# A modulation front in three groups of rows on TensorE, with an extra product per unit and a reordered start

## What is computed

```python
c_act = jax.nn.silu(c)
cc_act = jax.nn.silu(c_ctx)
mod = (c_act @ ada_w[l] + ada_b[l])[:, None, :]
sh1, sc1, g1, sh2, sc2, g2 = jnp.split(mod, N_MOD, axis=-1)
h = modulate(x, sh1, sc1)            # x * (1 + sc1) + sh1
mod_c = cc_act @ ada_w[l] + ada_b[l]
hc = modulate(x_ctx, csh1, csc1)     # the context tokens, layer 0 only
y, yc = even_mixer(h, hc, ...)       # h @ w_in, hc @ w_in, then attention
```

## Time and profile before

| what | value |
|---|---|
| time, median of 3 runs | 1842.48 us (1840.47 to 1844.92) |
| the profiled execution, its time | 1838.9 us |
| its span | 1837.0 us |
| TensorE busy | 1780.8 us, 97% of the span |
| VectorE / ScalarE / GpSimd busy | 1257.7 / 896.2 / 1003.9 us |
| mean granted TensorE clock | 0.992 of full |
| moved by DMA | 346.01 MB |

### The profile page before, as it was taken

One profiled execution on the slowest core, in us unless ns is written; L12 is line 12 of the kernel. 1 busy time (PEld: TensorE's weight loads), 2 busy tenths in 40 slices (PEclk: granted clock), 3 DMA queues, 4 the chain that ended last, 5 costly groups with the idle time before them and its releaser, 6 DMA issues.

```text
span 1837.0 us, 30955 instructions
## 1 busy us (share of the span) xinstructions
PE 1780.8 (97%) x10814; PEld 1532.3 (83%) x10814; DVE 1257.7 (68%) x2222; ACT 896.2 (49%) x1507; POOL 1003.9 (55%) x431
## 2 busy tenths in 40 slices
PE   5999899998999999999999999999999999999998
PEld 2847579987988887788879799999999988888887
DVE  6587657878548877515433369978889957777776
ACT  3034744455436554443354546665555555455553
POOL 4033146444666543585438768877777744444443
PEclk8999999999999999999999999999999999999999
DMA  8787247876565555553325455544444455555554
GB/s 328 252 306 252 93 138 231 278 267 217 198 230 174 188 186 169 172 172 119 111 92 175 160 179 181 182 162 166 162 161 161 161 188 191 193 194 194 194 194 161
DMA packets 95323, 346.01 MB, mean 188 GB/s; under 512 B 10544, under 2 KB 12032, under 8 KB 94592
## 3 DMA queue, kind: packets, MB, share of 16 engines
q1 hardware_dynamic: 78048, 283.67, 45.9%
q10 hardware_dynamic: 17184, 61.11, 9.5%
HBM read 343.66 MB, written 1.08 MB: 188 GB/s over the span
## 4 chain that ended last, share of the span: by engine, by line
PE 81%; DVE 8%; DMA 4%; issue 3%; ACT 2%; POOL 2%; ACTq 0%; DVEq 0%; SPq 0%; POOLq 0%
PE ps L635 27%; PE ps L570 24%; PE ps L582 6%; PE ps L588 3%; DMA ring<-stream 2%; PE ps L705 2%; PE ps L554 2%; PE ps L791 2%; POOL ring_lo L515 2%; PE ps L1023 2%; PE ps L858 2%; PE ps L805 2%; PE ps L1290 1%; PE ps L615 1%; DVE hot_parts_b L2813 1%
## 5 line engine op out<-in xcount | busy, mean ns | idle before, releaser
L515 POOL TENSOR_TENSOR ring_lo<-ring,ring_hi 128x1024 fp32r<-128x1024 f32 x371 | 901.0, 2432 | 645.8 <-ACT ring_hi L509 644.6
L509 ACT ACTIVATE ring_hi<-ring 128x1024 fp32r<-128x1024 f32 x502 | 531.6, 1060 | 547.2 <-DMA ring<-stream 545.1
L570 PE MATMUL ps<-h_span,ring_hi 128*128 128x256 f32 x3168 | 415.9, 284 | 0.6 <-ACT ring_hi L509 0.6
L570 PEld LDWEIGHTS ps<-h_span,ring_hi 128*128 128x128 f32 x3168 | 396.4, 192 | 6.4 <-issue 4.2
L635 PE MATMUL ps<-ring_hi,e_pair 128*128 128x512 f32 x1024 | 253.6, 389 | 1.9 <-DVE e_pair L2854 1.9
L2854 DVE TENSOR_TENSOR e_pair<-arena,e_pair 128x256 fp32r<-128x256 f32 x128 | 174.6, 1364 | 100.2 <-ACT e_pair L1857 99.9
L635 PEld LDWEIGHTS ps<-ring_hi,e_pair 128*128 128x128 f32 x1024 | 192.1, 188 | 41.9 <-issue 2.3
L570 PE MATMUL ps<-h_span,ring_lo 128*128 128x256 f32 x1584 | 222.3, 283 | 0.4 <-POOL ring_lo L515 0.4
L570 PEld LDWEIGHTS ps<-h_span,ring_lo 128*128 128x128 f32 x1584 | 204.3, 192 | 0.8 <-POOL ring_lo L515 0.8
L515 DVE TENSOR_TENSOR ring_lo<-ring,ring_hi 128x1024 fp32r<-128x1024 f32 x141 | 179.2, 1272 | 37.6 <-ACT ring_hi L509 37.3
L635 PE MATMUL ps<-ring_hi,arena_r 128*128 128x512 f32 x672 | 175.8, 394 | 2.4 <-ACT ring_hi L509 2.4
(11 more groups left out here) (297 smaller groups left out, 2195.5 us busy)
## 6 DMA issues: line engine op xcount, KB each, us to landing
ring<-stream SPq DMA_DIRECT2D x540, 512.0 KB, 3.3
arena<-aside_w ACTq DMA_DIRECT2D x49, 512.0 KB, 4.6
late<-aside_w ACTq DMA_DIRECT2D x21, 512.0 KB, 4.7
resid<-aside_w ACTq DMA_DIRECT2D x10, 512.0 KB, 6.3
arena<-scale_w ACTq DMA_DIRECT2D x8, 512.0 KB, 14.7
arena<-ln_rows ACTq DMA_DIRECT2D x8, 512.0 KB, 5.3
arena<-gate_cols ACTq DMA_DIRECT2D x2, 1024.0 KB, 4.6
arena<-decay ACTq DMA_DIRECT2D x1, 1536.0 KB, 6.8
```

What stands on the lines that cost most here:

```text
L509: act.activation(ring_hi[:, s, :], ring[:, s, :], ACT.Copy).then_inc(hi_ready, 1)
L515: eng.tensor_tensor(ring_lo[:, s, :], ring[:, s, :], ring_hi[:, s, :], ALU.subtract).then_inc(lo_ready[s], 1)
L570: m = pe.matmul(ps[:, bank, 0:T], w[:, kc * P:(kc + 1) * P], x[:, kc, :], start=begin, stop=w is w_lo and kc == KC - 1)
```

## The change

It does the following, all of it in the first 60 us of the program.

- The stream has four more units of `ada_w` at its start (`EARLY_ADA` 8 to 12, 544 units in all), and `early_rows` runs three times: the third group makes the scale chunks 0 to 3. `scale_w` has four chunks instead of eight (4 to 7), all of them VectorE's; GpSimd's products and ScalarE's sums are gone.
- In `early_rows`, each of the first three units of a group is followed by one more product of 512 columns into bank 2, whose result nobody reads (L725 of the new file). `early_columns(g-1)` now stands inside the next group, between its second and third unit.
- ScalarE's queue asks for the identity table second, and for `x` and the four small tables before it waits for the condition rows. The remaining tables and the context are asked for after ScalarE has scaled its four chunks of `x`.
- `first_pair()` replaces the first two k_tile calls. It takes chunks 4 to 7 of unit 0, then the third `early_columns`, then chunks 4 to 7 of unit 1, then chunks 0 to 3 of both. Every chunk has its own signal (`h_act`, `h_dve` now count to 8, so later users of the two counts wait for 8 + 4r instead of 2 + 4r).
- VectorE makes 1 + scale for chunks 4 to 7 first and signals; the columns of the third group come after that, and then its own four chunks.
- `bias_row()` moves behind `first_pair()`.

```diff
@@ -51,11 +51,9 @@
 
 
 ADA_UNITS = 48
-EARLY_ADA = 8
-ASIDE = 2 * ADA_UNITS - 2 * EARLY_ADA
-SCALE_DVE = (0, 1, 2, 3, 4)
-SCALE_POOL = (5, 6, 7)
-SCALE_LOADS = (0, 5, 1, 6, 2, 3, 7, 4)
+EARLY_ADA = 12
+ASIDE = 2 * ADA_UNITS - 16
+SCALE_DVE = (4, 5, 6, 7)
 PROJ_TILES = [(0, 0), (0, 1), (1, 0), (1, 1), (2, 0), None, (3, 0), (3, 1), (4, 0), (4, 1)]
 FRONT_PROJ = len(PROJ_TILES)
 N_PROJ = 18
@@ -172,7 +170,8 @@
     return 4 * min(GROUPS, -(-4 * (k + 1) // 5))
 
 
-EARLY_BANKS = (4, 5)
+EARLY_BANKS = (4, 5, 4)
+COLUMN_BANKS = (6, 7, 3)
 B_MAPS = 2 * 8
 MAPS = B_MAPS + 2 * 4
 A_BANKS = (2, 3, 7, 0, 1)
...
@@ -711,25 +707,31 @@
 
 
             pe.wait_ge(cact_ready, 1)
-            def early_rows(g):
+            def early_rows(g, between=None):
 
                 b = EARLY_BANKS[g]
                 start_fill(b)
                 for k4 in range(4):
                     w = unit(FIRST_UNIT["ada0"] + 4 * g + k4)
+                    if k4 == 2 and between is not None:
+                        between()
                     for k2 in range(2):
                         kc = 2 * k4 + k2
                         m = pe.matmul(ps[0:2, b, :], cact[:, kc, :], w[:, k2 * 512:(k2 + 1) * 512],
                                       start=kc == 0, stop=kc == KC - 1)
                         if k2 == 0:
                             m.then_inc(units_begun, 1)
+                    if k4 < 3:
+                        pe.matmul(ps[0:2, 2, :], cact[:, 0, :], w[:, 0:512], start=True, stop=True)
                 m.then_inc(full[b], 1)
                 fills[b].add()
+                mark["early", g] = b, fills[b].n
 
             def early_columns(g):
 
-                pe.wait_ge(emptied[EARLY_BANKS[g]], fills[EARLY_BANKS[g]].now())
-                b = 6 + g % 2
+                b, fill = mark["early", g]
+                pe.wait_ge(emptied[b], fill)
+                b = COLUMN_BANKS[g]
                 start_fill(b)
                 for q in range(4):
                     m = pe.matmul(ps[:, b, 2 * q:2 * q + 2], early_row[0:2, g, q * P:(q + 1) * P],
@@ -737,15 +739,28 @@
                 m.then_inc(full[b], 1)
                 fills[b].add()
 
-            for g in range(EARLY_ADA // 4):
-                early_rows(g)
-                if g == 0:
-                    pe.wait_ge(ident_in, 16)
-                else:
-                    early_columns(g - 1)
-            early_columns(EARLY_ADA // 4 - 1)
-            pe.wait_ge(inputs, 16 * 4)
-            bias_row()
+            early_rows(0)
+            pe.wait_ge(ident_in, 16)
+            early_rows(1, lambda: early_columns(0))
+            early_rows(2, lambda: early_columns(1))
+
+            def first_pair():
+
+                ws = [unit(PROJ_UNIT[n]) for n in range(2)]
+                start_fill(4)
+                for part in range(2):
+                    for n in range(2):
+                        for kc in (range(4, 8), range(4))[part]:
+                            if n == 0:
+                                pe.wait_ge(h_act if part == 0 else h_dve, kc % 4 + 1)
+                            m = pe.matmul(ps[:, 4, n * T:(n + 1) * T], ws[n][:, kc * P:(kc + 1) * P], hcat[:, kc, T:2 * T],
+                                          start=n == 0 and kc == 4, stop=kc == 3, skip_group_check=True)
+                            if kc == (4, 0)[n]:
+                                m.then_inc(units_begun, 1)
+                        if part == 0 and n == 0:
+                            early_columns(2)
+                m.then_inc(full[4], 1)
+                fills[4].add()
 
             def rotate(t):
 
@@ -820,10 +835,16 @@
                     t, half = tile
                     pair = t != 2
                     if t == 2:
-                        pe.wait_ge(h_dve, 2)
-                        pe.wait_ge(h_act, 2)
-                    k_tile(PROJ_UNIT[n], lambda kc: hcat[:, kc, T if pair else 0:2 * T], 4 + t % 2, at=T * half,
-                           done=tile_done(n) is not None)
+                        pe.wait_ge(h_dve, 8)
+                        pe.wait_ge(h_act, 8)
+                    if n >= 2:
+                        k_tile(PROJ_UNIT[n], lambda kc: hcat[:, kc, T if pair else 0:2 * T], 4 + t % 2, at=T * half,
+                               done=tile_done(n) is not None)
+                    elif n == 0:
+                        first_pair()
+                        pe.wait_ge(ident_in, 16)
+                        pe.wait_ge(inputs, 16 * 4)
+                        bias_row()
                     if tile_done(n) in (1, 2):
                         rotate(t - 1)
                         head_squares(t - 1)
...
@@ -1341,48 +1360,33 @@
             def all_rows(src, k):
                 return bass.AP(src.tensor, src.offset + k * D, [[0, P], [1, D]])
 
-            def scale_load(k):
-                act.dma_start(scale_in[:, k, :], scale_w[k]).then_inc(scale_w_in[k], 16)
-
             act.dma_start(par[:, :], params).then_inc(params_in, 16)
+            act.dma_start(cst[:, 0:P], consts[:, 0:P]).then_inc(ident_in, 16)
             for c, dst in enumerate((c_all, cc_all)):
                 act.dma_start(dst, all_rows(c_rows, c)).then_inc(c_in[c], 16)
-            for k in SCALE_LOADS[:5]:
-                scale_load(k)
+            for n in range(len(SCALE_DVE)):
+                act.dma_start(scale_in[:, n, :], scale_w[n]).then_inc(scale_w_in[n], 16)
             act.wait_ge(params_in, 16)
             act.activation(cact[:, :, :], param("c", 0, 16).rearrange("p (k c) -> p k c", c=2),
                            ACT.Silu).then_inc(cact_ready, 1)
-            for k in SCALE_LOADS[5:]:
-                scale_load(k)
+            act.dma_start(h[:, :, :], x_t).then_inc(x_in, 16)
+            for dst, src in ((relb[0:32, :], rel_bias), (oneh[0:32, :], onehot), (dmask[0:8, :], dist_mask), (lamb, lam_in)):
+                act.dma_start(dst, src).then_inc(inputs, 16)
             for c, dst in enumerate((c_all, cc_all)):
                 act.wait_ge(c_in[c], 16)
                 act.activation(dst, dst, ACT.Silu).then_inc(c_all_ready, 1)
-            act.dma_start(cst[:, 0:P], consts[:, 0:P]).then_inc(ident_in, 16)
-            act.dma_start(h[:, :, :], x_t).then_inc(x_in, 16)
-            for dst, src in ((relb[0:32, :], rel_bias), (oneh[0:32, :], onehot), (dmask[0:8, :], dist_mask), (lamb, lam_in)):
-                act.dma_start(dst, src).then_inc(inputs, 16)
-
-            def scale_sums(n):
-
-                k = SCALE_POOL[n]
-                for c, src in enumerate((scale_out[k], scale_in[:, k, :])):
-                    act.wait_ge(scale_product, 2 * n + c + 1)
-                    act.activation(src, src, ACT.Copy, accum_out=mod[0][:, SC1 + k, c:c + 1]).then_inc(scale_sum, 1)
-
             def drain(b, dst, func=ACT.Copy, n=T, **kw):
                 act.wait_ge(full[b], drains[b].add())
                 act.activation(dst, ps[:, b, 0:n], func, **kw).then_inc(emptied[b], 1)
 
-            for g in range(EARLY_ADA // 4):
-                scale_sums(g)
-                act.wait_ge(full[EARLY_BANKS[g]], 1)
-                act.activation(early_row[0:2, g, :], ps[0:2, EARLY_BANKS[g], :], ACT.Copy).then_inc(
-                    emptied[EARLY_BANKS[g]], 1)
-            act.dma_start(z, ctx_t).then_inc(ctx_in, 16)
-            act.dma_start(cst[:, P:], consts[:, P:]).then_inc(consts_in, 16)
-            scale_sums(2)
-            drains[4].add()
-            drains[5].add()
+            def early_copy(g):
+
+                b = EARLY_BANKS[g]
+                act.wait_ge(full[b], drains[b].add())
+                act.activation(early_row[0:2, g, :], ps[0:2, b, :], ACT.Copy).then_inc(emptied[b], 1)
+
+            early_copy(0)
+            early_copy(1)
 
             n_var = Count()
 
@@ -1398,9 +1402,12 @@
             for c, src in enumerate((h, z)):
                 act.wait_ge((x_in, ctx_in)[c], 16)
                 for kc in range(4, KC):
-                    m = act.activation(hcat[:, kc, (1 - c) * T:(2 - c) * T], src[:, kc, :], ACT.Identity,
-                                       scale=sc1p[:, kc, c:c + 1], bias=mod[0][:, SH1 + kc, c:c + 1])
-                m.then_inc(h_act, 1)
+                    act.activation(hcat[:, kc, (1 - c) * T:(2 - c) * T], src[:, kc, :], ACT.Identity,
+                                   scale=sc1p[:, kc, c:c + 1], bias=mod[0][:, SH1 + kc, c:c + 1]).then_inc(h_act, 1)
+                if c == 0:
+                    act.dma_start(cst[:, P:], consts[:, P:]).then_inc(consts_in, 16)
+                    act.dma_start(z, ctx_t).then_inc(ctx_in, 16)
+                    early_copy(2)
 
             def on_all(rows, k):
                 return bass.AP(rows.tensor, rows.offset + k * D, [[0, P], [1, D]])
...
@@ -1953,21 +1958,32 @@
                 m = mod[l][:, at_col:at_col + n, 0]
                 return dve.tensor_tensor(m, m, param(f"ada_b{l}", at_col, n), ALU.add)
 
+            def scales(first):
+
```

(29 more changed lines are left out.)

43 lines of the change are left out of this document (16 added, 27 removed).

## The result

| what | before | changed |
|---|---|---|
| median of 13 runs each, same chip | 1842.48 us (1833.59 to 1846.57) | 1848.92 us (1844.02 to 1855.22) |
| ratio | | 1.0042, 95% interval 1.0029 to 1.0055 |
| profiled execution, its time and span | 1838.9, 1837.0 us | 1849.28, 1847.5 us |
| fourth projection unit ends | 57.23 us | 68.40 us |

The change makes the kernel 7.7 us slower by the ratio (0.42% of 1843; 5.3 to 10.1 by the interval; the two medians in the table differ by 6.4). The forecast was no change, and 1848.92 lies above the range. Behind the fourth projection unit the span has 1779.8 us before and 1779.1 after: in these two profiles the loss stands wholly in the front.

A forecast was written before the change was run, and what follows sets the result against it. TensorE, 97% busy, was taken as the bound, so only the fourth projection unit's end, 57.24 us, counted. Terms summed to 55.0, plus 1.5 for the stream: 0.7 us faster, 1838.2 for the execution, 1841.8 median, range 1838.0 to 1845.0.

The forecast's parts named there:

- stream term: Rows on TensorE: waiting for stream units 4 to 6, taken as 1.5 us, between 0 and 2.5.
- Unit 7 and later: Stream behind unit 6: these units have 6 to 7.7 us to arrive, so their waits cost nothing.
- The part on context and tables: ScalarE's queue: both asked for at about 38 to 39, context landing at 48.5 to 50.5, no cost in the sum.
- just covered: Unit 14, third projection unit: asked for near 40.5, wanted at 49.5, its like taking 8.4 us, so no wait.
- Rival B: Clock falls in gaps at units 4 to 6 and first pair; one drop 2.6 us slower, 1845.1; chance 0.13.
- case of two drops: Gaps at units 4 to 6 and first pair: second clock drop, 5.4 us slower, 1847.9; chance 0.04.
- ScalarE's copy is hidden by four projection products: Third turning, between two parts of the first pair: four projection products, 1.75 us, hide ScalarE's copy.
- The three waits that the forecast works out: TensorE ahead of units 4, 5 and 6: said to sum to about 2.0 us at most by the earlier latencies.
- the first group's end at 18.8: First group of rows on TensorE, starting at 6.54: predicted to end at 18.8 us.
- the removal of GpSimd's part worth nothing: VectorE's scale chunks: 1.22 instead of 3.35 us each, done near 32, no gain because TensorE's rows are later.
- the four scaled chunks hidden: Ahead of the pair's products: ScalarE's four chunks of 2.07 us and VectorE's four of 1.38 us are covered.
- the rest of the program, held to be fixed within 2 us: Stretch behind the fourth projection unit: same work in same order, length changing by no more than 2 us.

The follow-up runs named there:

- e1: Changed kernel with the requests for remaining tables and context moved behind ScalarE's third copy of a row; ratio to before 1.0012.
- e2: Changed kernel with the requests for remaining tables and context moved early, directly behind ScalarE's first copy of a row; ratio to before 1.0015.
- e10: The changed kernel repeated from the same code, with a second profile; ratio to before 1.0049.
- e5: Changed kernel with six more products of 512 columns at the head of first_pair, filling the stop; 1853.43 us, ratio to before 1.0055.
- e9: Same as e8 but with the context asked for ahead of the tables; 1838.60 us, ratio to before 0.9970.
- e3: Changed kernel with each of first_pair's two units waited for where it is first used, not both at its start; ratio to before 1.0024.
- e8: Changed kernel with units waited for apart, no extra products, third row in bank 5, tables and context asked for behind the third copy; ratio to before 0.9992.
- e4: Changed kernel without the nine extra products of 512 columns; ratio to before 1.0018.
- e11: Repeat of e7, built from the same code; ratio to before 0.9980.
- e7: Changed kernel with units waited for apart, no extra products, third row in bank 5, tables and context asked for behind the first copy; ratio to before 0.9983.
- e6: The kernel before with only the identity table asked for second on ScalarE's queue; ratio to before 0.9999.

## Why the prediction was wrong

Its own sum, term by term, ended at 56.5; the profile has 68.40.

| term | predicted | measured | off by |
|---|---|---|---|
| end of twelve units of rows, two turnings, stream term | 41.0 | 42.29 | +1.3 |
| wait ahead of the first pair | 0 | 5.78 | +5.8 |
| first pair and third turning | 7.8 | 12.49 | +4.7 |
| bias row and second pair | 7.7 | 7.84 | +0.1 |

**The step that failed** is the sentence "Unit 7 and later are asked for when ScalarE's queue has only `x` and tables left ... and have 6 to 7.7 us, so I cost them at nothing". It ranged over all units from 7 on and priced them by one latency, although the change puts 1.9 MB on the other queue in the middle of them. The part on context and tables had their moment right (38 to 39), and the transfer table had the price: a unit beside them takes 8.4 us. The unit that is asked for just then is 13, at 39.03, and had until 42.29, 3.3 us and not 6 to 7.7, because the pair waits at its head for both units. 8.4 less 3.3 is 5.1 of the 5.78: the rows shown sufficed. The forecast did look for this collision, but at the wrong unit: it found unit 14 "just covered". e1 and e2 show the cause by taking the collision away.

**The clock.** Rival B had the mechanism and part of the price (2.8 for one restart; 4.2 measured, since the clock stayed down for some 9 us of work instead of 5.5), but placed it in the gaps at units 4 to 6. In the first profile the one fall followed from the wait that was not seen. In e10, the same kernel, the clock fell after the gap at unit 4 as well, as B has it, and so it did in e1, e2, e5 and e9; its chance of 0.13 was low. Its case of two drops, 1847.9, came nearest to the result, with one of the drops in another place.

**"ScalarE's copy is hidden by four projection products"**: wrong. The products wait for the copy, since the bank is the same; 0.88 us in e1 and e2, covered by the longer stop in the changed kernel.

**Two waits in one.** The order of the instructions, shown ahead of the prediction, has `landed1,landed0` at the first product of the pair. The forecast did not price it. In e3, without it, the end is 6.4 us earlier and the time 3.3 us lower (7.7 against 4.4, the intervals overlap).

**The sum of the stream term.** The three waits that the forecast works out are 1.0, 0.6 and 0.9 us, which is 2.5 and not the 2.0 that it states; the term taken was 1.5.

What held: the first group's end at 18.8 (19.0); a gap ahead of the second group (2.08 against a term of 1.5 for three units, of which only unit 4 was late); the removal of GpSimd's part worth nothing, as far as the trace tells, for VectorE's chunks were done at 32.2 while the columns came at 37.9; and the four scaled chunks hidden. Two more things came out right by luck. The context was in time, but the stop had put off the moment at which it was wanted; in e8, without the stop, the sine product waits for 0.89 us. And the rest of the program, held to be fixed within 2 us, differs by 0.7 us between the two profiles compared but by up to 12 over all thirteen. Units 4 to 6 took 7.8, 7.3 and 6.2 us. The queues between 14 and 18 us, to be read with the earlier trace rows:

```profile
q10 hardware_dynamic: 336, 1.50, 91.5%
q1 hardware_dynamic: 44, 0.18, 11.2%
```

SyncE's queue got 0.18 of 1.68 MB, less than the third it had before. The Trainium skill (DMA: Bandwidth & Descriptors, Queues, rings and completion order) has each engine go round robin between the queues with work, a packet at a time; neither this stretch nor 0.01 of 0.79 MB at 39 to 42 us agrees with turns taken evenly. From 43 to 46 us it got 0.47 of 1.25 MB, which is nearer to that.

The nine extra products were priced at 7.8 us and took 8.6, and they bought 3.4 us less waiting (2.1 against 5.4 in e4) and in that profile no clock. The kernel without them, with the waits apart, a free bank, late requests and the context first (e9) is faster than before, so the plan of the change, rows for all twelve units on TensorE, was sound, and its details cost some 13 us.

## What to carry to other kernels

When a request is moved, write down which request of the other queue goes out next and how long that one has, and price each unit by its own neighbours, never a run of units by one latency. When a helper waits for several things at its head, ask what could already run on the first of them. A stop of TensorE can be paid twice, here 5.8 us as time and 4.2 in the work behind it, so look for every one before the clock is left out of a sum.

## What the runs showed of the hardware

- A 512 KB request right behind 1.9 MB on the other queue took 8.9 us (6.9 to 10.0 for the next request of the stream in e3, e4, e5, e8, e9 and e10), and its queue moved 0.01 MB in the first 3 us; without the 1.9 MB the same unit took 3.3 us (e1, e2). It was not slowed evenly: for some 4 us it was held back, and then its queue had 0.47 of 1.25 MB (43 to 46 us).
- Gaps of TensorE of like length did not act alike. After 2.08 us (changed), 2.61 (e4), 3.27 (e11), 3.47 (e7) and 3.54 (e8) the clock stayed at 1.00; after 2.36 (e5), 2.53 (e10), 2.59 (e2), 2.67 (e1), 3.02 (e9) and 3.60 (e6) it went to 0.50, and in e3 after one of 0.68 and one of 1.69. The fall can come when work has begun again: some 1 us later in e3, in e5 and at the second fall of e10. The length of a gap alone does not tell whether the clock falls. This was not settled further.
- After the falls the clock came back at different times: near 57, 9 us after work began again, in the changed kernel; in e4 a stop at the same place (6.29 us) was followed by a return some 4 us after work began.
- The same 10,700 TensorE instructions behind the front were busy for 1740.6 us in e3 and 1750.6 in e5, at mean granted clocks of 0.997 and 0.991. Two profiles can thus differ by 10 us in a stretch that no edit touched, and a front has to be judged by its own end.
